# Early expert tiles of the selection: from four-pass fp32 products to three rounded products with GpSimd subtractions, and 24 tiles instead of 20

## The reference

```python
def _peer(h, w_q, k1, k2, u_tab, v_tab):
    q = (h @ w_q).reshape(b, l, PEER_HEADS, 2, PEER_HALF)          # 8 heads
    s1 = einsum('blhc,hnc->blhn', q[..., 0, :], k1)                # 128 keys
    s2 = einsum('blhc,hnc->blhn', q[..., 1, :], k2)
    v1, i1 = lax.top_k(s1, 16);  v2, i2 = lax.top_k(s2, 16)
    cand_s = (v1[..., :, None] + v2[..., None, :])                 # 256 sums
    top_s, pos = lax.top_k(cand_s, 16)
    idx = take_along_axis(cand_i, pos);  g = softmax(top_s)
    u = take(u_tab, idx);  a = gelu(einsum('ted,td->te', u, h))
    return einsum('te,ted->td', g * a, take(v_tab, idx))
```

## Time and profile before

| | us |
|---|---|
| median of three runs | 2875.99 |
| profiled execution, its own time | 2878.01 |
| its span | 2876.2 |
| TensorE busy in it | 2805.0 |
| VectorE busy | 2078.1 |
| ScalarE busy | 1155.8 |
| GpSimd busy | 80.7 |

### The profile page before, as it was taken

One profiled execution on the slowest core, in us unless ns is written; L12 is line 12 of the kernel. 1 busy time (PEld: TensorE's weight loads), 2 busy tenths in 40 slices (PEclk: granted clock), 3 DMA queues, 4 the chain that ended last, 5 costly groups with the idle time before them and its releaser, 6 DMA issues.

```text
span 2876.2 us, 51321 instructions
## 1 busy us (share of the span) xinstructions
PE 2805.0 (98%) x19732; PEld 2428.3 (84%) x19740; DVE 2078.1 (72%) x3925; ACT 1155.8 (40%) x1799; POOL 80.7 (3%) x96
## 2 busy tenths in 40 slices
PE   9999999999999899999999999999999999999997
PEld 7876998886996579998999999876999999999986
DVE  6866886766774569997666666774999766666677
ACT  4514554523552432344444444431223444444443
POOL 0012000022000000000000000000000000000000
PEclk9999999999999999999999999999999999999999
DMA  5205883304883134425555555653442555555564
GB/s 204 102 17 221 332 308 125 113 18 185 330 318 116 59 118 165 145 78 192 188 185 185 186 189 190 243 196 132 167 153 77 179 185 184 188 189 190 190 232 156
DMA packets 79284, 498.35 MB, mean 173 GB/s; under 512 B 9264, under 2 KB 13744, under 8 KB 22320
## 3 DMA queue, kind: packets, MB, share of 16 engines
q1 hardware_dynamic: 70080, 477.77, 45.8%
q10 hardware_dynamic: 9072, 18.72, 1.9%
HBM read 485.97 MB, written 10.49 MB: 173 GB/s over the span
## 4 chain that ended last, share of the span: by engine, by line
PE 93%; DVE 4%; issue 1%; ACT 1%; POOL 1%; DMA 0%; DVEq 0%; ACTq 0%; SPq 0%; POOLq 0%
PE bank L909 24%; PE bank L897 24%; PE bank L936 7%; PE bank L1937 6%; PE bank L2128 5%; PE bank L2166 4%; PE bank L2175 4%; PE bank L573 2%; PE bank L722 2%; PE bank L775 2%; PE bank L1980 1%; PE bank L2108 1%; PE bank L2217 1%; PE bank L1925 1%; PE bank L651 1%
## 5 line engine op out<-in xcount | busy, mean ns | idle before, releaser
L909 PE MATMUL bank<-peer_pass_high,peer_pass_hidden 128*128 128x512 f32 x1472 | 488.2, 393 | 0.0
L897 PE MATMUL bank<-peer_pass_high 128*128 128x256 f32 x1456 | 409.1, 281 | 0.0
L897 PE MATMUL bank<-hT_r,peer_pass_high 128*128 128x256 f32 x1456 | 408.6, 281 | 0.0
L897 PE MATMUL bank<-peer_pass_high,ring_r 128*128 128x256 f32 x1456 | 408.6, 281 | 0.0
L1001 DVE TENSOR_TENSOR ring_r<-ring,peer_pass_high 128x1024 fp32r<-128x1024 f32 x184 | 225.4, 1225 | 229.6 <-ACT peer_pass_high L1605 229.6
L909 PEld LDWEIGHTS bank<-peer_pass_high,peer_pass_hidden 128*128 128x128 f32 x1472 | 276.7, 188 | 55.8
L1605 ACT ACTIVATE peer_pass_high<-ring 128x1024 fp32r<-128x1024 f32 x184 | 195.1, 1060 | 315.7 <-DMA ring<-in_experts 314.9
L909 PE MATMUL bank<-ring_r,peer_pass_hidden 128*128 128x512 f32 x736 | 289.2, 393 | 0.0
L897 PEld LDWEIGHTS bank<-peer_pass_high 128*128 128x128 f32 x1456 | 274.4, 188 | 8.7 <-DVE ring_r L1001 0.5
L897 PEld LDWEIGHTS bank<-hT_r,peer_pass_high 128*128 128x128 f32 x1456 | 274.6, 189 | 7.4
L897 PEld LDWEIGHTS bank<-peer_pass_high,ring_r 128*128 128x128 f32 x1456 | 274.5, 189 | 0.0
(11 more groups left out here) (408 smaller groups left out, 5665.2 us busy)
## 6 DMA issues: line engine op xcount, KB each, us to landing
ring<-in_experts SPq DMA_DIRECT2D x256, 1024.0 KB, 4.8
ring<-in_w SPq DMA_DIRECT2D x137, 1024.0 KB, 4.8
sb<-in_w_mod SPq DMA_DIRECT2D x48, 1024.0 KB, 6.7
sb<-spill SPq DMA_DIRECT2D x36, 256.0 KB, 5.0
spill<-sb ACTq DMA_DIRECT2D x10, 512.0 KB, 6.8
sb<-in_ln ACTq DMA_DIRECT2D x8, 512.0 KB, 4.9
spill<-sb ACTq DMA_DIRECT2D x32, 128.0 KB, 1.8
sb<-in_post ACTq DMA_DIRECT2D x4, 512.0 KB, 4.4
```

The lines of the kernel that those rows point to most:

```text
L897: m = pe.matmul(ps[u][:, 0:S], w, h[:, kt, :], start=(kt, i) == (0, 0), stop=(kt, i) == (KT - 1, 2))
L909: m = pe.matmul(ps[4 + 2 * tb + half][:, :], g[:, t], w, start=False, stop=False, skip_group_check=True)
```

## The change

The early tiles of the selection are no longer plain fp32 products. For each slot (two tiles) ACT makes the rounded high half (`act_early_high`), GpSimd subtracts it from the slot (`pool_early_low`), and TensorE forms three rounded products through `pe_three`. There are 24 such tiles in each expert layer instead of 20, so the expert loop has 88 instead of 92 and the late part 40 instead of 36. `gates(1)` stands before tile 18 instead of 14, the early slots no longer start one ring place later, and the last four gelu results are kept in the space of the keys, whose groups of `W` follow earlier (`EARLY_FREE` 26 instead of 32).

```diff
-EARLY_SELECT, EARLY_BUILD = 20, 16
+EARLY_SELECT, EARLY_BUILD = 24, 16
+SELECT_SLOTS = EARLY_SELECT // 2
...
-        return (pos + (seg[:5] == "early") + FF_RING * (seg == "ff")) % RING
+        return (pos + FF_RING * (seg == "ff")) % RING
...
-GATES_BEFORE = 14
+GATES_BEFORE = 18
...
     def early_up(t):
-        w = slot(k, pe, f"early{l}", t // 2)
+        s = t // 2
+        r = STREAM.ring(f"early{l}", s)
+        pe.wait_ge(k.early_low, early_split(l, s))
         b = J.give(pe, ("eu", t), l)
         for kt in range(KT):
-            m = pe.matmul(ps[b][:, 0:S], w[:, (t % 2) * D + kt * P:(t % 2) * D + (kt + 1) * P], k.hT[:, kt, :],
-                          start=kt == 0, stop=kt == KT - 1)
+            w = slice((t % 2) * D + kt * P, (t % 2) * D + (kt + 1) * P)
+            m = pe_three(pe, ps[b][:, 0:S], (k.q_high[early_high(s)][:, w], k.ring_r[r][:, w]),
+                         (k.PX.hh[:, kt, :], k.h_low[:, kt, :]), kt == 0, kt == KT - 1)
...
+def act_early_high(k, a, l, s):
+    r = STREAM.ring(f"early{l}", s)
+    a.wait_ge(k.weights_loaded[r], STREAM.loaded(f"early{l}", s))
+    a.activation(k.q_high[early_high(s)], k.ring[r], ACT.Copy).then_inc(k.early_high, 1)
+
+def pool_early_low(k, p, l):
+    for s in range(SELECT_SLOTS):
+        r = STREAM.ring(f"early{l}", s)
+        p.wait_ge(k.early_high, early_split(l, s))
+        p.tensor_tensor(k.ring_r[r], k.ring[r], k.q_high[early_high(s)].bitcast(F32), ALU.subtract).then_inc(k.early_low, 1)
...
+        if t % 2 == 0 and 4 <= t // 2 + 2 < SELECT_SLOTS:
+            act_early_high(k, a, l, t // 2 + 2)
...
+        if h >= PH - 2:
+            act_early_high(k, a, l, h - (PH - 2))
     gates(0)
+    act_early_high(k, a, l, 2)
     early_up(0)
     score(PH - 1)
-    for t in range(1, EARLY_SELECT - 1):
+    early_up(1)
+    act_early_high(k, a, l, 3)
+    for t in range(2, EARLY_SELECT - 1):
...
             for n in range(min(upto, 5) - 1):
                 pool_ln_rstd(k, p, st2, n)
+                if n % 2 == 0 and n + 2 < upto:
+                    pool_early_low(k, p, n // 2)
```

More of the change, by code:

```diff
@@ L1757 @@
 W_GROUPS = S // 4
-BUILD_TURNS, EARLY_FREE = (EARLY_BUILD - 1) // 3, 32
+BUILD_TURNS, EARLY_FREE, EARLY_HERE = (EARLY_BUILD - 1) // 3, 26, 20
 SCORES, SCORE_BANK = 4, 4
@@ L1875, in plan_memory2 @@
     k.sel = r.take(TB, 3, PH, TOPK)
-    k.early = r.take(EARLY_SELECT, S)
+    k.early = r.take(EARLY_HERE, S)
+    k.early_last = shaped(k.keys[:, 0:(EARLY_SELECT - EARLY_HERE) * S], EARLY_SELECT - EARLY_HERE, S)
     k.early2 = [k.sb[:, k.late + KT * S + i * S:k.late + KT * S + (i + 1) * S] for i in range(3)]
@@ L2157, in pe_peer @@
     base = l * W_GROUPS
+    last_early = J.at[("eu", EARLY_SELECT - 1)] % NBANK
+    last_early = 4 * (last_early - 4) if last_early >= 4 else last_early
     for g in range(W_GROUPS):
-        if g == J.at[("eu", EARLY_SELECT - 1)] % NBANK:
+        if g == last_early:
             J.evac(pe, ("eu", EARLY_SELECT - 1), l)
@@ L2438, in query_high, with early_high, early_split @@
     return i % 4
+def early_high(s):
+    return query_high(s + 3)
+def early_split(l, s):
+    return l * SELECT_SLOTS + s + 1
+def act_early_high(k, a, l, s):
[7 more added lines that the diff above has]
+        p.tensor_tensor(k.ring_r[r], k.ring[r], k.q_high[early_high(s)].bitcast(F32), ALU.subtract).then_inc(k.early_low, 1)
 def query_split(l, i):
@@ L2728, in early_up @@
         b = J.take(a, "act", ("eu", t), l)
-        a.activation(k.early[:, t, :], k.psum[b][:, 0:S], ACT.Gelu).then_inc(J.read["act"], 1)
+        to, n = (k.early, t) if t < EARLY_HERE else (k.early_last, t - EARLY_HERE)
+        a.activation(to[:, n, :], k.psum[b][:, 0:S], ACT.Gelu).then_inc(J.read["act"], 1)
         if t % 4 == 3:
@@ L2732, in early_up @@
             a.dma_start(k.spill[bass.ds(t // 4, 1)].rearrange("a p n -> (a p) n"),
-                        k.early[:, t - 3:t + 1, :].rearrange("p a b -> p (a b)")).then_inc(k.early_out, 16)
+                        to[:, n - 3:n + 1, :].rearrange("p a b -> p (a b)")).then_inc(k.early_out, 16)
+        if t % 2 == 0 and 4 <= t // 2 + 2 < SELECT_SLOTS:
+            act_early_high(k, a, l, t // 2 + 2)
     J.evac(a, ("xt", 2), l)
@@ L2967, in build @@
         k.early_out = sem("early_out")
+        k.early_high, k.early_low = sem("early_high"), sem("early_low")
         k.early2_out = [sem(f"early2_out{i}") for i in range(4)]
```

## The result

The changed kernel takes 2929.5 us (median of 4 runs, 2925.95 to 2932.79) beside 2876.1 us before (2875.21 to 2878.34): ratio 1.0186, 95% interval 1.0172 to 1.0199. It is 53.4 us slower; 26 us were forecast. The profiled execution took 2927.55 us, 49.5 us more than the one of before (2878.01).

A forecast was written before the change was run, and what follows sets the result against it. TensorE bounds the kernel, with VectorE level in the selections. 2878.0 - 22.6 (tiles) + 26.0 + 19.4 (stops) + 3.4 (clock) = 2904.2 us, with the profiled execution 2.0 us above the median: 2902 us; range 2878 to 2935 us.

The forecast's parts named there:

- The path over `gates(1)`, slot 11 and tile 22: Selection: late VectorE holds ACT in `gates(1)`, delaying slot 11's copy; TensorE waits for tile 22; one more 3.6 us turn.
- TensorE's account of -22.6 us: Expert loop loses four tiles (22.4 us), late part gains four (11.1 us): 11.3 us less per layer, 22.6 in both.
- The lower clock at the restart: TensorE restarts at 1.2 instead of 2.4 GHz after the selection's long stop: 1.7 us per layer, 3.4 in all.
- the price of one subtraction: GpSimd's 2048-column subtraction in the selection: 3.6 us, from a line through instructions of 12, 384 and 768 columns.
- 26.0 and 19.4 us of stops: TensorE's stops in the selections of layers 0 and 1: VectorE's delay less TensorE's slack and the shorter last tile.
- the walk: Replay of VectorE's, ACT's and TensorE's selection lists at 3.6 us a subtraction: VectorE 26.7 and 20.7 us late.
- full turn: In the selection, a VectorE two-SBUF-operand instruction stands for one whole GpSimd subtraction: 3.6 us each.
- The first rival: Same mechanism in the selections at 4.4 us a subtraction: 40.2 and 32.7 us at the transposes, 2930 us; chance 0.25.
- instructions with one SBUF operand are free: In the selection, VectorE instructions with one SBUF operand never wait for GpSimd; delay nothing.
- No blocking: GpSimd's subtractions pass beside VectorE in the selection without blocking it; TensorE's account stands alone: 2852 us; chance 0.14.
- GpSimd as the bound: In the selection GpSimd needs 6.1 us a slot against TensorE's 5.68 us: 2955 us or above; chance 0.05.
- The fair share: In the selection GpSimd and VectorE share bandwidth; large products take twice as long: 2878 us, no change; chance 0.08.

The follow-up runs named there:

- no_sub: The change with GpSimd's subtraction cut to 2 of 2048 columns, TensorE reading the high half twice: 2851.8 us.
- micro: Separate kernel without the model: GpSimd instructions timed alone and paired with one VectorE instruction; subtracting two different tensors of 2048 columns took 4492 ns.
- one_tensor: The change with GpSimd's subtraction replaced by a product of the high half with itself, same 2048 columns: 2902.5 us.
- gates22: The change with ScalarE taking up the second block of gates before tile 22 instead of tile 18: 2925.2 us.
- mixed28: Against the change: 28 early tiles, only slots 3 to 11 split, the other ten tiles plain fp32, second gates before tile 20: 2863.2 us.
- mixed_4_9: The change's 24 tiles with only slots 4 to 9 split, the other tiles one fp32 product each: 2865.0 us.

## Why the prediction was wrong

**Right:** the kernel before had two level engines, and what delays VectorE delays everything. GpSimd's subtraction and a VectorE instruction of two SBUF operands exclude each other to the end, first come first served: shown by the turns of 4.40, 3.40 and 1.1 us for GpSimd instructions of 4.5, 3.6 and 1.26 us. The path over `gates(1)`, slot 11 and tile 22 came as described. TensorE's account of -22.6 us was measured by itself (746.4 against 735.1 us behind the second selection, and no_sub). ScalarE's copies cost nothing (no_sub). The lower clock at the restart costs (1.54 - 0.66) + (3.93 - 2.84) = 2.0 us a layer; 1.7 were forecast.

**Wrong: the step "the price of one subtraction".** It took 3.6 us; the instruction takes 4.49 us alone and 4.52 us at the least here. The line through 12, 384 and 768 columns was straight, but none of its three instructions reads two long tensors: the 768-column one multiplies `od` with itself, the 384-column one has one value for 64 columns, the 12-column one a repeated scale. Those are the 1.67 ns line of micro, which does end at 3.60 us; the subtraction is on the 2.10 ns line. A straight line through three points says nothing on a fourth of another form, and the code of these three lines would have told it. The Trainium skill (GPSIMD Engine Reference, Performance versus the Vector engine) gives 4.497 us for an addition of this length; the 4.492 us of micro agree with it, so where the rows spoke against the page they spoke of another form.

This is the term of the sum that was mis-sized: 26.0 and 19.4 us of stops stood in it, and the traces show 40.6 and 34.9 us of delay on VectorE, where the walk behind them had 26.7 and 20.7. A price too low by 0.9 us became a delay too small by some 14 us in a layer, because it entered twice. Each full turn costs 4.40 us, against 3.40 us in one_tensor, and there are eight full turns instead of six in layer 0 and seven instead of five in layer 1 (counted in the traces of the change and of one_tensor): a longer subtraction makes the first gates last longer, and so more later subtractions find the gates still going. The parts of turns are nearly equal in layer 0, 5.8 and 6.2 us. The first rival, the same walk with 4.4 us, had 40.2 and 32.7 us at the transposes and 2930 us; with the clock, 41.9 and 34.4 us stand beside the measured 41.9 and 35.8, and 2930 beside 2929.5 us. The forecast had this case at 0.25, against 0.48 for its own. The measured time lies inside the stated range only because the range took in this rival; the forecast's own range, 2893 to 2912 us, doesn't hold it.

**Too narrow: "instructions with one SBUF operand are free".** Maximum and reduction are, but micro shows that copy, cast and product with a constant wait; in the change it shows in a cast of 1.40 us instead of 0.23 (L2512). The Trainium skill (SBUF — State Buffer, Who interferes with whom) names copy, cast and `tensor_scalar` as able to contend and the reduction as not; micro agrees on all of them. In the change the cast adds 1.2 us in layer 1 and nothing in layer 0.

**The other rivals.** No blocking (2852 us) fell with the trace; its time is what no_sub shows. GpSimd as the bound (2955 us) fell: TensorE waits long for it once a layer, and then for a copy that ScalarE made late. The fair share (2878 us) fell with the result, and with micro, where GpSimd's product isn't lengthened at all.

Open: in gates22 VectorE is delayed by 1.3 and 2.1 us more than in its walk (36.1 and 28.5 us). The cast of L2512, which is lengthened there in both layers, is 1.1 and 1.2 us of this; the rest wasn't looked for. Nor is it settled whether mixed28 is better than mixed_4_9.

## What to carry to other kernels

An engine that works off the critical path can still stop the one on it. Before work is given to GpSimd, write down in which order VectorE's instructions come, mark those that wait for GpSimd (two SBUF operands, copies, casts, products with a constant), and put GpSimd's instructions beside the others; if they can't be placed, cut them short, since the price is the length of one turn times the number of turns. Take a price only from an instruction with the same kinds of operands, and walk the list again with the upper bound, because the number of turns grows with their length.

## What the runs showed of the hardware that was not expected

- On GpSimd a product of one tensor with itself takes 1.67 ns a column, and a product or subtraction of two different tensors 2.10 ns (3.598 and 4.492 us for 2048 columns). A product with repeated values costs what the first costs, measured at 384 columns (0.83 us).
- A VectorE copy, cast or product with a constant, 1024 fp32 columns in SBUF, waits for GpSimd's instruction (4.15 us, with 3.6 us of waiting) like a product of two tensors; the maximum, the reduction and a product with a PSUM operand don't (1.23, 1.22 and, for 512 columns, 0.69 us).
- GpSimd's instruction is never lengthened by a VectorE instruction that comes behind it (4.46 us in all eight pairs), and by the alternation of the change at most by one VectorE product (5.62 us).
